# Latent attention of a two-block layer: one visit for a pair's value products, and the scaling of the probabilities moved to ScalarE

## What is computed

```python
def blocked_causal_attention(q, k, v):
    ...
    def one_block(i):
        ...
        s = jnp.einsum('bqhd,bkhd->bhqk', qb, k).astype(jnp.float32) * scale
        qpos = start + jnp.arange(ATTN_Q_BLOCK)
        s = jnp.where(qpos[:, None] >= key_pos[None, :], s, -jnp.inf)
        p = jax.nn.softmax(s, axis=-1).astype(v.dtype)
        return jnp.einsum('bhqk,bkhd->bqhd', p, v)
...
        g_ssd, g_mla = jnp.split(jax.nn.sigmoid(gates + gate_b[i]), 2, axis=-1)
        x = x + (g_ssd * y_ssd + g_mla * y_mla) @ w_o[i]
```

## Time and profile before

| what | value |
|---|---|
| time, median of 3 runs | 1615.64 us (1615.55 to 1615.93) |
| the profiled execution | 1615.44 us, of which span 1613.6 us |
| TensorE busy | 1593.2 us (99%) |
| VectorE busy | 1039.7 us (64%) |
| ScalarE busy | 741.2 us (46%) |
| GpSimd busy | 660.7 us (41%) |
| attention loop, 946 to 1160 us of the span: TensorE, VectorE, ScalarE busy | 211.37, 170.89, 111.25 of 214.00 us |
| a middle pair, from one value visit at i = 0 to the next (1062.95 to 1090.85 us) | 27.90 us |
| TensorE's longest wait in the last pair's turns (for line 2057, before unit 63) | 0.77 us |
| granted TensorE clock | 1.00 |

### The profile page before, as it was taken

The page is one execution under the profiler, slowest core; times in us unless marked ns, Lnnn a source line. Parts: engine busy times, 40 slices in busy tenths (PEclk is TensorE's granted clock), DMA queues, the critical chain, the costliest instruction groups (busy, mean ns, idle before and its releaser), DMA issues.

```text
span 1613.6 us, 22213 instructions
## 1 busy us (share of the span) xinstructions
PE 1593.2 (99%) x7824; PEld 1265.6 (78%) x7843; DVE 1039.7 (64%) x1662; ACT 741.2 (46%) x1287; POOL 660.7 (41%) x307
## 2 busy tenths in 40 slices
PE   7999999999999999999999999999999999999999
PEld 6688767777888888777778878777788888888887
DVE  6699586677436877677775078887586765566100
ACT  5423465565345654555553245454534443434220
POOL 4344563332454244244464332222254354444442
PEclk9999999999999999999999999999999999999999
DMA  6243222213333244211113322121333233323331
GB/s 213 79 118 96 88 80 65 66 54 142 92 105 104 58 138 135 79 53 53 51 55 104 91 66 66 53 66 53 112 95 102 79 104 92 102 92 103 93 98 60
DMA packets 40371, 143.40 MB, mean 89 GB/s; under 512 B 4501, under 2 KB 5173, under 8 KB 39901
## 3 DMA queue, kind: packets, MB, share of 16 engines
q1 hardware_dynamic: 37600, 131.96, 26.7%
q10 hardware_dynamic: 2684, 10.27, 1.8%
HBM read 137.63 MB, written 4.58 MB: 88 GB/s over the span
## 4 chain that ended last, share of the span: by engine, by line
PE 84%; issue 9%; POOL 3%; DVE 3%; ACT 2%; DMA 0%; POOLq 0%; SPq 0%; DVEq 0%; ACTq 0%
PE bank L798 18%; PE bank L800 18%; PE bank L799 18%; PE bank L1457 4%; PE bank L1459 4%; PE bank L1458 4%; POOL w_lo L658 2%; PE bank L1343 2%; PE bank L850 1%; PE bank L851 1%; PE bank L849 1%; PE bank L1364 1%; PE bank L1352 1%; PE bank L1246 1%; PE bank L1252 1%
## 5 line engine op out<-in xcount | busy, mean ns | idle before, releaser
L658 POOL TENSOR_TENSOR w_lo<-w_raw,w_hi 128x1024 fp32r<-128x1024 f32 x241 | 592.5, 2461 | 916.4 <-ACT w_hi L1487 779.1
L798 PE MATMUL bank<-u_hi,w_hi 128*128 128x512 f32 x768 | 324.0, 422 | 1.6 <-ACT gm L2042 0.8
L1487 ACT ACTIVATE w_hi<-w_raw 128x1024 fp32r<-128x1024 f32 x197 | 207.3, 1056 | 210.7 <-PE bank L800 169.5
L800 PE MATMUL bank<-u_hi,w_lo 128*128 128x512 f32 x768 | 300.6, 391 | 0.0
L799 PE MATMUL bank<-u_lo,w_hi 128*128 128x512 f32 x768 | 299.5, 390 | 0.0
L798 PEld LDWEIGHTS bank<-u_hi,w_hi 128*128 128x128 f32 x768 | 144.4, 188 | 45.9 <-issue 13.7
L800 PEld LDWEIGHTS bank<-u_hi,w_lo 128*128 128x128 f32 x768 | 144.1, 188 | 31.5
L799 PEld LDWEIGHTS bank<-u_lo,w_hi 128*128 128x128 f32 x768 | 144.7, 188 | 30.3 <-issue 2.4
L1457 PE MATMUL bank<-u_hi,w_hi 128*128 128x512 f32 x288 | 112.0, 389 | 0.0
L1458 PE MATMUL bank<-u_lo,w_hi 128*128 128x512 f32 x288 | 112.0, 389 | 0.0
L1459 PE MATMUL bank<-u_hi,w_lo 128*128 128x512 f32 x288 | 112.0, 389 | 0.0
(11 more groups left out here) (480 smaller groups left out, 3405.2 us busy)
## 6 DMA issues: line engine op xcount, KB each, us to landing
w_raw<-weights SPq DMA_DIRECT2D x243, 512.0 KB, 3.6
xt<-x_t SPq DMA_DIRECT2D x8, 256.0 KB, 6.4
hank<-bias_dram ACTq DMA_DIRECT2D x8, 256.0 KB, 4.3
xt<-x_t ACTq DMA_DIRECT2D x1, 2048.0 KB, 9.0
h_dram<-h_res ACTq DMA_DIRECT2D x1, 2048.0 KB, 7.7
h_res<-h_dram ACTq DMA_DIRECT2D x1, 2048.0 KB, 7.5
out<-h_res SPq DMA_DIRECT2D x8, 256.0 KB
p_val<-p_t ACTq DMA_DIRECT2D x1, 512.0 KB, 11.2
```

Of the source, the lines that this page charges most:

```text
L658: pool.tensor_tensor(w_lo[:, j, :], w_raw[:, j, :], w_hi[:, j, :].bitcast(F32), ALU.subtract).then_inc(w_lo_ready, 1)
L798: pe.matmul(o, hi, xh, start=(i == 0), stop=False)
L800: mm = pe.matmul(o, lo, xh, start=False, stop=(i == n - 1))
L1487: act.activation(w_hi[:, c % RING, :], w_raw[:, c % RING, :], ACT.Copy).then_inc(w_hi_ready, 1)
```

## The change

`pair_values` now takes a first and an end block of queries and goes by blocks of keys: for each block of keys j and head s one matmul over all blocks of queries from j on, so 512, 384, 256 and 128 columns, 8 matmuls instead of 20. The seven pairs with a successor get one visit, at i = 0 of the next pair, ahead of `head_turn`; the last pair gets one for blocks 0 to 2 at i = 6 and one for block 3 at the end. `turned_x` becomes one tile of 20 blocks in an order in which each such range lies together, and the odd head's blocks stand reversed in bank 6. The scaling of line 2859 leaves VectorE, which only takes the reciprocal and raises `x_inverse`; ScalarE does the scaling as a copy with a scale for each partition, as the first thing of its unit (`head_scaled(n + 1)`), ahead of `mix_gate`. The factor 0.5 goes into the copies of the values.

```diff
--- before.py
+++ after.py
@@ -477,9 +477,13 @@
 
         v_tok = at("v_tok", 104, [P, NT, XH * VD])
         o_raw = at("o_raw", 120, [P, KD, S])
-        probs_x = at("probs_x", 186, [P, 4, S])
-        turned_x = [[at(f"turned_x{s}{ti}", kb, [P, (ti + 1) * P]) for ti, kb in enumerate(kbs)]
-                    for s, kbs in enumerate(((49.5, 201, 198, 194), (55.5, 48.5, 199.5, 196)))]
+        probs_x = [at(f"probs_x{i}", kb, [P, w]) for i, (kb, w) in
+                   enumerate(((48.5, 3 * P), (190, 3 * P), (186, S), (188, S)))]
+        turned_x = at("turned_x", 192, [P, 20, P])
+
+        def turned_block(s, j, ti):
+
+            return 16 - 4 * j + ti if s else 3 * j + ti
         gm = at("gm", 170, [P, KD, S])
         q_s = at("q_s", 56, [P, 4, S])
         k_s = at("k_s", 64, [P, 4, S])
@@ -601,6 +605,7 @@
         x_out = sem("x_out")
         gates_used = sem("gates_used")
         x_scaled = sem("x_scaled")
+        x_inverse = sem("x_inverse")
         krope_summed = sem("krope_summed")
         act_in = sem("act_in")
         act_sg = sem("act_sg")
@@ -1349,21 +1354,22 @@
                 if n:
                     pe.wait_ge(x_turned_out, n)
                 for j in range(ti + 1):
-                    mm = pe.transpose(bank[6][:, j * P:(j + 1) * P], probs_x[:, n % 4, j * P:(j + 1) * P], ident[:, :])
+                    k = ti - j if h % 2 else j
+                    mm = pe.transpose(bank[6][:, k * P:(k + 1) * P], probs_x[n % 4][:, j * P:(j + 1) * P], ident[:, :])
                 mm.then_inc(x_turn, 1)
 
-            def pair_values(p, half):
-
-                pe.wait_ge(x_turned_out, 8 * p + 4 * half + 4)
-                if p and not half:
+            def pair_values(p, first, end):
+
+                pe.wait_ge(x_turned_out, 8 * p + 2 * end)
+                if p and not first:
                     pe.wait_ge(x_out, p)
-                for ti in (2 * half, 2 * half + 1):
-                    for j in range(ti + 1):
-                        for s in range(2):
-                            h = 2 * p + s
-                            mm = pe.matmul(bank[7][64 * s:64 * s + 64, ti * P:(ti + 1) * P],
-                                           v_tok[:, j, h * VD:(h + 1) * VD], turned_x[s][ti][:, j * P:(j + 1) * P],
-                                           start=(j == 0), stop=(j == ti))
+                for j in range(end):
+                    q = max(j, first)
+                    for s in range(2):
+                        h, b = 2 * p + s, turned_block(s, j, q)
+                        mm = pe.matmul(bank[7][64 * s:64 * s + 64, q * P:end * P], v_tok[:, j, h * VD:(h + 1) * VD],
+                                       turned_x[:, b:b + end - q, :].rearrange("p a b -> p (a b)"), start=(j == 0),
+                                       stop=(j == end - 1))
                 mm.then_inc(x_sum, 1)
 
             def of_kn(k):
@@ -1417,12 +1423,14 @@
                 if more and i == 2:
                     key_sums(p + 1)
                     query_sums(2 * p + 3)
+                if p and i == 0:
+                    pair_values(p - 1, 0, NT)
+                if not more and i == 6:
+                    pair_values(p, 0, NT - 1)
                 head_turn(n)
                 if last:
                     column_tile(st["mix_gate"][2 * p + 1], of_u2, part=(i, i + 1))
-                if n and n % 4 == 0:
-                    pair_values((n - 4) // 8, (n - 4) // 4 % 2)
-            pair_values(XH // 2 - 1, 1)
+            pair_values(XH // 2 - 1, NT - 1, NT)
 
 
             column_tiles(st["mla_out"], lambda k: (o_hi[k][:, :], o_lo[k][:, :]), n_lo["o"] - KD, pair=True)
@@ -1544,13 +1552,13 @@
             def tile_done(t):
                 act.wait_ge(dense_done, t["full"])
 
-            def rows_out(tiles, dst, mine=(0, 2)):
+            def rows_out(tiles, dst, mine=(0, 2), scale=1.0):
                 for c, s in tiles[0]["parts"][:-1]:
                     if s == CH * P // S - 1:
                         split_weights(c)
                 for i in mine:
                     tile_done(tiles[i])
-                    act.copy(dst(i), bank[tiles[i]["bank"]][:, :]).then_inc(act_freed, 1)
+                    act.mul(dst(i), bank[tiles[i]["bank"]][:, :], scale).then_inc(act_freed, 1)
                 after(tiles[0])
 
             def sigmoid_of(t):
@@ -2046,18 +2054,26 @@
                 h, ti = heads[n]
                 W = (ti + 1) * P
                 act.wait_ge(x_max, n + 1)
-                act.activation(probs_x[:, n % 4, 0:W], probs_x[:, n % 4, 0:W], ACT.Exp, bias=x_cols[:, 1, n:n + 1],
+                act.activation(probs_x[n % 4][:, 0:W], probs_x[n % 4][:, 0:W], ACT.Exp, bias=x_cols[:, 1, n:n + 1],
                                scale=-1.0, accum_out=x_cols[:, 2, n:n + 1]).then_inc(x_probs, 1)
+
+            def head_scaled(n):
+                W = (heads[n][1] + 1) * P
+                act.wait_ge(x_inverse, n + 1)
+                act.activation(probs_x[n % 4][:, 0:W], probs_x[n % 4][:, 0:W], ACT.Copy,
+                               scale=x_cols[:, 3, n:n + 1]).then_inc(x_scaled, 1)
 
             def head_turned(n):
                 h, ti = heads[n]
                 act.wait_ge(x_turn, n + 1)
                 if n >= 8:
-                    act.wait_ge(x_sum, n // 4 - 1)
-                act.copy(turned_x[h % 2][ti][:, :], bank[6][:, 0:(ti + 1) * P]).then_inc(x_turned_out, 1)
+                    act.wait_ge(x_sum, n // 8)
+                first, step = (turned_block(1, ti, ti), 4) if h % 2 else (ti, 3)
+                act.copy(turned_x[:, first:first + step * ti + 1:step, :],
+                         bank[6][:, 0:(ti + 1) * P].rearrange("p (a b) -> p a b", b=P)).then_inc(x_turned_out, 1)
 
             def values_out(half):
-                rows_out(st["v"][4 * half:4 * half + 4], lambda i: v_tok[:, i, half * S:(half + 1) * S])
+                rows_out(st["v"][4 * half:4 * half + 4], lambda i: v_tok[:, i, half * S:(half + 1) * S], scale=0.5)
 
             act.wait_ge(krope_summed, 1)
             query_squares(0)
@@ -2074,9 +2090,12 @@
             act.wait_ge(latent_consts, 2)
             head_probs(0)
             head_probs(1)
+            head_scaled(0)
             for n, (h, ti) in enumerate(heads):
                 p, i = divmod(n, 8)
                 more = 2 * p + 2 < XH
+                if n + 1 < len(heads):
+                    head_scaled(n + 1)
                 if i == 0:
                     mix_gate(2 * p)
                 if more and i == 4:
@@ -2103,7 +2122,7 @@
             mix_gate(XH - 1)
             for i in range(4, KD - 1):
                 act.activation(o_hi[i][:, :], o_raw[:, i, :], ACT.Copy).then_inc(hi_ready, 1)
-            act.wait_ge(x_sum, XH)
+            act.wait_ge(x_sum, XH // 2 + 1)
             act.activation(o_hi[KD - 1][:, :], bank[7][:, :], ACT.Copy).then_inc(hi_ready, 1)
             after(st["mix_gate"][XH - 1])
             act.dma_start(r_back[:, :], r_dram).then_inc(h_back, 16)
@@ -2261,10 +2280,10 @@
                 dve.wait_ge(dve_freed, frees[0])
                 dve.sem_inc(ev_used, 1)
 
-            def rows_out(tiles, dst):
+            def rows_out(tiles, dst, scale=1.0):
                 for i in (1, 3):
                     dve.wait_ge(dense_done, tiles[i]["full"])
-                    free(dve.tensor_copy(dst(i), bank[tiles[i]["bank"]][:, :]))
+                    free(dve.tensor_scalar(dst(i), bank[tiles[i]["bank"]][:, :], scale, None, ALU.mult))
 
             n_part, n_added = [0], [0]
 
@@ -2847,7 +2866,7 @@
                 if n >= 4:
                     dve.wait_ge(x_turn, n - 3)
                 dve.wait_ge(x_logits, n + 1)
-                dve.tensor_tensor_reduce(out=probs_x[:, n % 4, 0:W], in0=bank[3 + n % 3][:, 0:W],
+                dve.tensor_tensor_reduce(out=probs_x[n % 4][:, 0:W], in0=bank[3 + n % 3][:, 0:W],
                                          in1=mask_x[:, S - W:S], scale=r_qk[:, h // 2 % 2, q:q + 1], scalar=3e38,
                                          op0=ALU.add, op1=ALU.min, accum_out=x_cols[:, 1, n:n + 1]).then_inc(x_max, 1)
 
@@ -2855,12 +2874,10 @@
 
                 W = (heads[n][1] + 1) * P
                 dve.wait_ge(x_probs, n + 1)
-                link(dve.reciprocal(x_cols[:, 3, n:n + 1], x_cols[:, 2, n:n + 1]))
-                dve.tensor_scalar(probs_x[:, n % 4, 0:W], probs_x[:, n % 4, 0:W], x_cols[:, 3, n:n + 1], 0.5,
-                                  ALU.mult, ALU.mult).then_inc(x_scaled, 1)
+                dve.reciprocal(x_cols[:, 3, n:n + 1], x_cols[:, 2, n:n + 1]).then_inc(x_inverse, 1)
 
             def values_out(half):
-                rows_out(st["v"][4 * half:4 * half + 4], lambda i: v_tok[:, i, half * S:(half + 1) * S])
+                rows_out(st["v"][4 * half:4 * half + 4], lambda i: v_tok[:, i, half * S:(half + 1) * S], scale=0.5)
 
             def gate_used(g):
                 dve.wait_ge(act_freed, st["mix_gate"][g]["freed"][1])
@@ -2909,7 +2926,7 @@
```

(4 more changed lines are left out.)

## The result

The changed kernel takes 1646.5 us (1645.57 to 1648.06, five runs) against 1615.83 us: ratio 1.0192, 95% interval 1.0181 to 1.0203. It was forecast slower, at 1633.0 us, with a range up to 1641.5. The direction was right and the amount was not: 30.7 us lost where 17.4 were worked out.

The account below looks back on a forecast made before the run. TensorE was taken as the bound, busy 1593.2 of 1613.6 us. Terms 18.8 - 2.5 - 0.1 + 1.2 = +17.4 on 1615.44 gave 1632.8, with the median 0.2 above: 1633.0 us, range 1628 to 1641.5.

Parts of the forecast that it names:

- The new wait: At i = 4, TensorE's gate product comes 3.90 us after the key spread instead of 1.21, in seven pairs: +18.8 us.
- The clock: Rival, 12 in 100: TensorE's 2.8 us gap at i = 4 lowers its clock, six slower matmuls each time: +10, so 1643.
- The products: Value products in one visit instead of two save 0.35 us a pair, seven times: -2.5 us; last pair -0.1.
- The last pair: In the last pair, scalings added to a nearly full ScalarE make TensorE wait: +1.2 us, bounds 0 and 3.
- What VectorE is spared: 64 scalings leave VectorE; taken as no gain, at most the 5.3 us TensorE waits before the key spread.
- The prediction's own test: The prediction is wrong if i = 4's gate product follows the spread within 1.3 us, or matmuls after the gap are 0.63 long.
- The reciprocal: Rival, 5 in 100: at i = 4 it ends before ScalarE's weight conversion, leaving only the products' gain: 1613.0 us.
- ScalarE's queue: Rival, 10 in 100: with 64 scalings it is late elsewhere too, losing 0.7 us a pair: +5, so 1638.
- The wide products: Rival, 1 in 100: the two heads' value products don't overlap in the array, 2 more us a pair.

Follow-up runs that it names:

- the two swaps: Changed kernel with one swap each: ScalarE's gate read ahead of the scaling, 1618.17 us; VectorE's reciprocal ahead of the key products at i = 4, 1620.18 us.
- The filled gap: Changed kernel plus 11 unused matmuls of 512 columns on TensorE between key spread and gate tile: 1633.32 us.
- the products alone: Changed kernel with the scaling and the factor 0.5 back on VectorE, one value visit kept: 1619.54 us.
- The scaling alone: Kernel before with only the scaling on ScalarE and the factor 0.5 in the value copies, two old visits kept: 1638.66 us.
- five fillers: Changed kernel plus 5 unused matmuls on TensorE right behind the key spread, instead of 11: 1633.32 us.
- the longer pair: Changed kernel plus two unused matmuls (0.46 us) at i = 5 of seven pairs: 1638.81 us.

## Why the prediction missed

- **The new wait: right.** From spread to gate product 3.98 instead of 1.21 us, so 2.77 where 2.69 was worked out, seven times: 19.4 instead of 18.8. The place and the chain were as said: each of the two swaps that cuts it takes back over 26 us. One term was too small: the scaling of 384 columns takes 0.61 us instead of 0.50, nearer to the 512 columns of the earlier trace rows than to the row of its own size.
- **The clock: the step that failed.** The prediction gave the fall of the clock 12 in 100, since a gap of 2.8 us "is nearer to 1.54", and put it at nothing in its sum. The filled gap shows what it was worth: 13.2 us. The range did not hold it either: the case was priced at 1643 and the range ended at 1641.5. The price was mis-sized as well, six slow matmuls of the earlier trace rows or 1.4 us after each of seven gaps (taken from their lengths, 0.63 for 0.40; the starts, 0.43 apart for 0.23, would have given 1.2). Six gaps were followed by a slow stretch. It cost 1.4 us in the first pair, 1.6 in the two near 31.8 us and 2.8 in the two near 33.05, in which it lasted to the end of the second gate part. From the last spread to the output projection it was 2.8 again (34.84 us against 32.08 with the gap filled), in all 13.0. The reasoning took the two rows as ends of a scale and the nearer one as the answer. But the two rows leave open everything between 1.54 and 9.39 us, and 2.8 lies there. With the price measured here the case would have been at 1646.
- **The products: right in their place, wrong by themselves.** In the changed kernel they save 0.44 us a pair (0.35 forecast, with 0.38 as its upper bound). But the prediction didn't name what covers VectorE when the visit at i = 4 goes. In the changed kernel it is the wait itself, in which VectorE gets ahead. With the wait gone and the scaling on VectorE that cover is gone too, and the products alone cost 3.9 us.
- **The last pair: right to 0.2 us.** From the last spread to the output projection the kernel before takes 28.39 us and the one with the filled gap 32.08. Of the 3.69 more, 2.77 are the seventh wait; 0.92 are left, where 1.2 - 0.1 - 0.35 = 0.75 was forecast. The scaling alone makes the stretch behind the last gate product 0.5 us longer (17.20 for 16.68), or 0.7 beside the one visit (18.29 for 17.57), and 0.3 stand before it at the gate read (1.12 for 0.83): 0.8 to 1.0 where 1.2 was said.
- **What VectorE is spared: nothing**, as taken. The wait before the spread is 5.3 us as before.
- **Sum.** 1633.0 forecast without the clock, 1633.3 measured with the gap filled. That it fits so closely is partly luck: the waits cost 0.6 us more than forecast, and the products saved 0.09 us a pair, some 0.6 in all, more. The prediction's own test, "if the matmuls after the gap are 0.63 long", is what the trace shows.
- **The rivals.** The reciprocal was not in time. ScalarE's queue does run late in units 4 to 6, but only once the gap is repaired: TensorE waits 0.2 to 0.5 us a pair there, and the pairs are 0.3 to 0.7 us over the 27.45 expected. The wide products overlap as in the earlier trace rows: the visit takes 2.30 us.

## What to carry to other kernels

Before work is moved to an engine with time to spare, look at what stands behind it in that engine's queue: here one scaling of 0.6 us, put ahead of a read that frees a bank and itself waiting for a result that another engine makes late, cost 2.8 us each time. When a forecast has TensorE idle for some microseconds, price the lower clock as a case in the range, or put work into the gap that can be done there. And work that is saved may have been cover for an engine that is late beside it; try it on its own before counting on it.

## What was not expected of the hardware

- TensorE's clock went to its lower level after idle stretches of 2.9 and of 2.1 us inside a dense loop, never after 1.5 (seven gaps of 1.54 us in the profiled run with five fillers, clock 1.00 in all four), and not always: the same gap of 2.89 us brought it down six times of seven in the changed kernel, whose pairs have 30.2 us without a slow stretch, and once of seven in each of the two profiled runs with pairs of 30.7 us. What decides between them stays open; only the longer pair was tried.
- Two VectorE instructions from SBUF to SBUF (on-chip memory) took 1.86 and 2.48 us beside GpSimd's subtraction, and 0.48 and 0.68 without it. Which instruction is hit depends on the order: with one out of the way the next is held.
